# Cross attention and experts: the second tile's softmax and values behind the first tile's outputs, and an earlier first query

## The reference, cut to what matters

```python
def mem_cross_attention(hn, mem_n, wq, wkv, wo):       # 4 heads of 256
    q = hn @ wq;  k, v = split(mem_n @ wkv, 2)
    p = softmax(einsum('bshd,bmhd->bhsm', q, k) * 256 ** -0.5)
    o = einsum('bhsm,bmhd->bshd', p, v).reshape(bsz, seq, D_MODEL)
    return o @ wo

def peer_ffn(hn, wq, subkeys, u_tab, v_tab):           # 8 heads, 2 x 128 subkeys of width 128
    q = (hn @ wq).reshape(T, 8, 2, 128)
    s = einsum('thpd,hpkd->thpk', q, subkeys)
    s1, i1 = top_k(s[:, :, 0], 16);  s2, i2 = top_k(s[:, :, 1], 16)
    top_s, pos = top_k(s1[..., :, None] + s2[..., None, :], 16)   # over the 256 pairs
    idx = (i1 * 128 + i2) at pos;  gate = softmax(top_s)
    act = gelu(einsum('td,thkd->thk', x, u_tab[idx]))
    return einsum('thk,thkd->td', gate * act, v_tab[idx])

h = h + mem_cross_attention(rms_norm(h), mem_n, ...)
h = h + peer_ffn(rms_norm(h), ...)
```

## Time and profile before

| | |
|---|---|
| median of 3 runs | 3084.23 us |
| lowest, highest | 3083.57, 3088.27 us |
| the profiled execution | 3088.53 us, span 3086.8 us |
| mean granted PE clock | 0.938 |
| PE, weight loads, DVE, ACT, POOL busy | 85%, 62%, 69%, 35%, 19% of the span |
| moved by DMA | 810.85 MB; gathers 536.90 MB |

### The profile page before, as it was taken

One profiled execution on the slowest core, in us unless ns is written; L12 is line 12 of the kernel. 1 busy time (PEld: TensorE's weight loads), 2 busy tenths in 40 slices (PEclk: granted clock), 3 DMA queues, 4 the chain that ended last, 5 costly groups with the idle time before them and its releaser, 6 DMA issues. The chain is left out here.

```text
span 3086.8 us, 36100 instructions
## 1 busy us (share of the span) xinstructions
PE 2616.6 (85%) x13122; PEld 1901.4 (62%) x13122; DVE 2116.7 (69%) x4141; ACT 1090.1 (35%) x1973; POOL 599.8 (19%) x547
## 2 busy tenths in 40 slices
PE   8988999998899999899887676668999897667675
PEld 7957998895799797788543222225888653222222
DVE  6457664646766567453889888866664789888875
ACT  4355444435444365444212111113644321112111
POOL 0000000000000000000445444441000254444442
PEclk9999999999999999999998888888999998888888
DMA  6422554552355443143999999997434799999996
GB/s 252 170 96 96 176 184 141 205 175 72 110 181 186 145 153 135 70 164 130 392 427 415 427 426 427 426 426 308 156 122 157 298 425 420 427 426 427 427 426 282
DMA packets 112498, 810.85 MB, mean 263 GB/s; under 512 B 12736, under 2 KB 12736, under 8 KB 14272
## 3 DMA queue, kind: packets, MB, share of 16 engines
q0 software_dynamic: 73728, 536.90, 41.4%
q1 hardware_dynamic: 38592, 271.63, 24.6%
HBM read 807.44 MB, written 1.05 MB: 262 GB/s over the span
## 5 line engine op out<-in xcount | busy, mean ns | idle before, releaser
L3336 PE MATMUL ps<-arena 128*128 128x512 f32 x912 | 533.3, 737 | 240.4 <-ACT arena L3232 236.9
L166 DVE TENSOR_TENSOR ring_low<-ring,parts 128x2048 fp32r<-128x2048 f32 x216 | 492.0, 2291 | 323.9 <-ACT parts L160 320.3
L457 PE MATMUL ps<-parts,parts 128*128 128x256 f32 x2528 | 570.3, 283 | 13.4 <-DVE ring_low L166 10.0
L3336 PEld LDWEIGHTS ps<-arena 128*128 128x128 f32 x912 | 205.4, 235 | 553.9 <-ACT arena L3232 318.6
L457 PE MATMUL ps<-parts,ring_low 128*128 128x256 f32 x1824 | 513.1, 281 | 0.0
L160 ACT ACTIVATE parts<-ring 128x2048 fp32r<-128x2048 f32 x216 | 410.5, 1913 | 270.4 <-PE ps L465 109.5
L465 PE MATMUL ps<-parts,parts 128*128 128x512 f32 x1344 | 439.5, 396 | 7.3 <-DVE ring_low L166 5.3
L457 PEld LDWEIGHTS ps<-parts,parts 128*128 128x128 f32 x2528 | 428.6, 189 | 16.4 <-issue 10.8
L3059 POOL DMA_INDIRECT arena<-in_experts,stage_index x276 | 327.8, 1188 | 536.8 <-PE ps L3336 253.9
L3107 DVE CUSTOM_DVE_ANT_0 arena<-arena 128x1024 f32<-128x1024 f32 x276 | 334.1, 1227 | 95.7 <-DMA arena<-in_experts,stage_index 92.9
L3336 PE MATMUL ps<-ring,arena 128*128 128x512 f32 x616 | 313.0, 645 | 96.8 <-ACT arena L3232 94.2
(11 more groups left out here) (490 smaller groups left out, 2971.5 us busy)
## 6 DMA issues: line engine op xcount, KB each, us to landing
ring<-in_stream SPq DMA_DIRECT2D x249, 1024.0 KB, 4.8
arena<-in_experts,stage_index POOLq DMA_INDIRECT x276
ring<-in_experts,stage_index POOLq DMA_INDIRECT x236
gain_row<-in_gain_rows SPq DMA_DIRECT2D x4, 512.0 KB, 5.9
arena<-in_mem SPq DMA_DIRECT2D x2, 1024.0 KB, 5.6
arena<-in_stream SPq DMA_DIRECT2D x2, 1024.0 KB, 8.5
par<-in_params SPq DMA_DIRECT2D x4, 386.0 KB, 5.0
x<-in_x SPq DMA_DIRECT2D x1, 1024.0 KB, 6.3
```

Of the source, the lines that this page charges most:

```text
L166: dve.tensor_tensor(k.ring_low[v % SLOTS], whole, self.high_of(v).bitcast(F32), ALU.subtract).then_inc(self.ph.sem("chunk_split"), 1)
L457: last = pe.matmul(self.ps[:, 2 * pair + f // 2, (f % 2) * T:(f % 2 + 1) * T], w[:, f * P:(f + 1) * P], x[:, k, :], start=(k == 0 and i == ...
L3336: last = pe.matmul(k.ps[:, bank + n, :], diag[:, s % ROWS, :], rows[row_of[s]][:, D + n * BLK:D + (n + 1) * BLK], start=(s % SLOTS_PER_TOK ...
```

## The change

It applies to both layers.

- On PE the scores, the turn and the values of tile 1 move behind work of tile 0: the scores of tile 1 come after the values of tile 0, its turn inside `outputs(0)`, its values after `outputs(0)` and half of the query product. The query product of tile 0 (`ask_first`, `ask`) stands around the values of tile 1, no longer between blocks of `outputs(1)`; `first_scores` comes after 2 blocks of `outputs(1)` instead of 7.
- ACT and DVE follow: exponentials, maximum and scaling of tile 1 stand behind the result of tile 0 and its third chunk of weights, and the first tile's norm stands in `cross_attention` in front of the result of tile 1.
- Behind the outputs PE asks the second half of the quarter for tile 0 alone, then turns tile 1, and asks the whole quarter for tile 1 in one piece. Before, it turned tile 1, asked the second half for both tiles, then the first half for tile 1.
- On ACT the rest of tile 0's query and the turned copies of tile 1 stand ahead of the squares of tile 1.
- PSUM banks for the turned x go by tile now, and some tiles of the arena lie elsewhere.

```diff
     def bank(self, i, m):
-        at = (i % 2) * T + m * P
-        return self.kern.ps[:, 4 + i // 2, at:at + P]
+        return self.kern.ps[:, 4 + 2 * m + i // self.HALF, (i % self.HALF) * P:(i % self.HALF + 1) * P]
...
 def cross_attention(...): tensor
                 for kt in range(KT):
-                    if (m, n, kt) in expert_early:
-                        expert_early[m, n, kt](pe)
+                    if (m, n, kt) == (0, 1, 2):
+                        turn(1)
+                    if (m, n, kt) == (0, 1, 4):
+                        early.turn_first(pe)
+                    if (m, n, kt) == (1, 0, 2):
+                        early.first_scores(pe)
...
         scores(0)
-        scores(1)
         k.linear_group(pe, ph, lv, (mem_high, mem_low), False, None, split, 0)
         turn(0)
-        turn(1)
         k.linear_group(pe, ph, lv, (mem_high, mem_low), False, None, split, 1)
-        pe.wait_ge(ph.sem("v_copied"), 2)
         values(0)
+        scores(1)
+        outputs(0)
+        early.ask_first(pe)
         values(1)
-        for m in range(MT):
-            outputs(m)
+        early.ask(pe)
+        outputs(1)
...
 def cross_attention(...): scalar, from the exponentials
+        exps(0)
+        split.high_for(act, lv, 0)
+        take_values(0)
+        take_turned(0)
+        split.high_for(act, lv, 1)
+        take_values(1)
+        out_high(0)
+        split.high_for(act, lo, 0, 1)
+        exps(1)
         split.high_for(act, lo, 1, 0)
         k.root_table(act)
+        early.scalar_first(act)
+        take_turned(1)
+        early.scalar_second(act)
+        out_high(1)
...
 def cross_attention(...): vector, from the maximum
+        maximum(0)
+        split.low_for(dve, lv, 0)
+        scale(0)
+        split.low_for(dve, lv, 1)
+        out_low(0)
+        maximum(1)
+        split.low_for(dve, lo, 0, 1)
+        scale(1)
+        early.vector_first(dve, link)
         split.low_for(dve, lo, 1, 0)
+        early.vector_second(dve, link)
+        out_low(1)
...
+class Early:
+    def vector_first(self, dve, link):
+        self.first_added(dve, 0)
+        link(dve.memset(self.z.index, 0.0))
+        self.norm.begin_mean(dve, link)
+    def vector_second(self, dve, link):
+        self.first_added(dve, 1)
+        self.norm.mean(dve, link, 0)
+        self.norm.finish(dve, link, 0)
+    def scalar_first(self, act):
+        self.norm.half_squares(act, 0)
+    def scalar_second(self, act):
+        self.norm.make_whole(act, 0, 0)
+        self.norm.half_squares(act, 1)
+        self.norm.make_whole(act, 0, 1)
+        self.norm.root(act, 0)
+    def ask_first(self, pe):
+        self.k.linear_piece(..., range(0, 4), range(0, 2), self.norm, None, toks=slice(0, P), first=False)
+        self.norm.turn(pe, 0, 1)
+    def ask(self, pe):
+        self.k.linear_piece(..., range(4, KT), range(0, 2), self.norm, "query_parts", toks=slice(0, P), first=False)
...
 def experts(...): scalar
         copy_scores(0, [0, 1])
-        norm.squares(act)
+        rest_of_query()
         norm.make_whole(act, 1, 0)
         norm.make_whole(act, 1, 1)
+        norm.squares(act)
+        copy_scores(0, [2, 3])
         norm.root(act, 1)
         exponentials(0)
-        rest_of_query()
-        copy_scores(0, [2, 3])
         second_tile_query()
...
 def experts(...): tensor
-        pe.wait_ge(ph.sem("scores_copied"), 1)
+        pe.wait_ge(norm.x_added, 3)
+        queries(0, fs=range(2, 4), done="query_parts", toks=first_tile, frees=False)
         norm.turn(pe, 1, 0)
         norm.turn(pe, 1, 1)
-        queries(0, fs=range(2, 4), done="query_parts", frees=False, after=KT)
         some_scores(0, range(2, 4), 2)
-        queries(0, fs=range(0, 2), toks=second_tile, frees=True, first=False, after=KT)
+        queries(0, toks=second_tile, first=False, after=KT)
         some_scores(1, range(0, 4), 3)
```

102 lines of the change are left out of this document (39 added, 63 removed).

## The result

The changed kernel took 3100.43 us (median of 6 runs, 3096.64 to 3102.09) beside 3084.36 for the kernel before (6 runs). The ratio is 1.0047, with a 95% interval of 1.0037 to 1.0057: 11 to 18 us slower. The forecast was 3091.6 us, its range ended at 3096. The direction was right and the size was not.

A forecast was written before the change was run, and what follows sets the result against it. It took the DMA stream of expert gathers as the bound, with buffer releases hanging on PE's first sum and DVE. Lateness of 2 x 3.7 = 7.4 us on the 3084.2 us median gave 3091.6 us; 8-in-10 range 3081 to 3096.

The forecast's parts named there:

- First gather 2.3 us nearer, outputs 1.2 us later: Scores to outputs on PE: first scores and first gather 2.3 us earlier (1.5 to 3), outputs of tile 1 end 1.2 later.
- DVE's mean 3.7 us late: Behind the outputs: DVE's mean of tile 1 waits for ScalarE's squares, at 1479.2 instead of 1475.54; bounds 2.5 and 5 us.
- PE's first sum at 1496.5: Start of expert row sums on PE: late with DVE's first weights, 1496.5 instead of 1492.77, after about 11 us idle.
- The hole: DMA stream before the eleventh gather's data: a gap of about 4 us, with 2 or 3 more around 1516 to 1524.
- Eleven gathers must wait for PE's first sum: Gather buffers: freeing those for gathers nine and ten 3.6 us early is worth nothing, as eleven gathers wait anyway.
- Nothing gives it back: Rest of each expert stage: DMA share stays 1.01, so the nineteenth gather's 3.7 us lateness is the stage's lateness.
- My upper bound of 5 us for the mean: DVE's mean of tile 1: at most 5 us late, if the outputs end 1 us later still.
- The earlier start: Rival: the first gather's earlier start sets the stage's end, each stage 2.3 us shorter, 3079.6 us; chance 0.13.
- The slow clock: Rival: PE's half clock lasts longer after the pause, up to 2.5 us more a layer, 3096.6 us; chance 0.10.
- Partly absorbed: Rival: the eleventh to eighteenth gathers catch up, 1 to 3 us a layer come back, middle 3087.6 us; chance 0.25.

The follow-up runs named there:

- squares_first: Changed kernel with ScalarE's squares of tile 1 ahead of the copy of tile 0's remaining query: 3086.52 us (1.0005) on chip 13, 3093.93 on chip 7.
- tail_before: Changed kernel's first half, with PE's and ScalarE's order of the kernel before behind the outputs of tile 1: 3085.54 us, 0.9998.
- warm: Changed kernel with 16 idle matmuls in PE's pause ahead of the first row sums: 3094.34 us, 1.0031.
- turns_first: Changed kernel with the two turns of tile 1 ahead of tile 0's remaining query on PE: 3093.41 us, 1.0020.
- root_early: Changed kernel with ScalarE's squares and square root of tile 1 ahead of the copy of tile 0's remaining query: 3087.46 us, 1.0006.
- add_behind: root_early with the pairs of the first unit ahead of the second half of tile 1's sum on DVE: 3087.26 us, 1.0006.
- add_behind_padded: add_behind with one harmless one-column copy a layer added on ScalarE: 3086.47 us, 1.0005.
- squares_late: Changed kernel with ScalarE's squares behind the copies of tile 0's last scores and tile 1's query: 3103.74 us (1.0057) on chip 13, 3115.36 on chip 7.

## Why the prediction was wrong, step by step

- **First gather 2.3 us nearer, outputs 1.2 us later.** Measured 2.1 and, from S to the query behind them, 69.3 instead of 67.9 us: 1.4. Right.
- **DVE's mean 3.7 us late.** This is the step that failed. The mechanism was right: ScalarE in strict order, squares behind the query's copy and the turned copies, and DVE's wait named <-ACT L710 in the trace. But the mean stood 6.9 us late (S + 80.1 instead of 73.3). I let the copy start when PE's query ended. It started 3.3 us later, by the held signal, a term that the sum had at nothing. Less these 3.3, the lateness is 3.6 us, the forecast's term. Why the signal is held stays open.
- **PE's first sum at 1496.5.** 1497.94 in an execution that began 1.2 us earlier: against S 6.4 us late instead of 3.7. PE's pause in front of it was 8.6 and 10.2 us, where some 11 were forecast. From the first gather to the nineteenth it took 59.6 us, not 57.
- **The hole.** Forecast at 4 us and 2 or 3 more, less the 2.3 us of earlier start. Measured 8.0 and 9.0 us less stream than before over the same 57 us. (An earlier sentence of the prediction, "Eleven gathers must wait for PE's first sum", is a slip: by the earlier trace rows the eleventh and those behind it wait.)
- **Nothing gives it back.** True of the two layers' sum at large doses (the rule of 2L less 2 us): the sums were 2 x 6.4 us late, the time 14.5 us longer. For one layer it isn't shown, as layer 0 took 4.7 us more and layer 1 8.8. For small doses it isn't either: squares_first's sum was 1.7 us late in each layer and its time moved by 1.5 us in all, but its interval (0.9996 to 1.0014) holds 3.4 us as well as nothing.
- **The rivals.** The earlier start is refuted by tail_before. The slow clock was real (6.04 us for the first sums, 3.70 when kept busy), but it did not last longer than before by more than the kernel before varies, and warm did not show its gain in time. "Partly absorbed" pointed the wrong way.
- **The range** ended at 3096. It took the copy's release as certain, so it had no term for a wait that the trace of before does not show. My upper bound of 5 us for the mean would have needed to be 7.

That the direction came out right is no luck, as the order alone costs time; that the term for it fits to 0.1 us is an inference from one subtraction. With the signal on time, the mean's lateness would then have been the forecast's. The changed kernel itself never ran on chip 13, so that it would have come near 3091 there is an inference, from turns_first (3093.4, squares 77.1 behind S) and from what the signal costs squares_first (7.4 us). That the order alone costs time is shown: turns_first had no held signal and was 1.0020, 1.0010 to 1.0030, while squares_first on the same chip was 1.0005, 0.9996 to 1.0014.

No version beat the kernel before: the best five, tail_before, squares_first on chip 13, root_early, add_behind and add_behind_padded, are all within 0.1% of it.

## What to carry to other kernels

Before you start a stage earlier, ask what frees the buffers of its second round: here the first gather could come 2.1 us earlier for nothing, since the eleventh waited for a sum that waited for the end of the outputs. On an engine in strict order, put what another engine waits for (squares and root) ahead of what hangs on a third engine's signal: with the signal held on one and the same chip, that made 1.0006 of 1.0039. Look for every such product, for the exponentials left behind the copy took what DVE won next. And when a wait is released by nothing that the trace names, try the same program on a second chip before looking for the cause in the program.

## What the hardware showed that I had not expected

- On four of the five numbered chips, and in the changed kernel's first profile, ScalarE got the signal of the query's matmuls up to 3.4 us after their modelled end, at a fixed moment 11.5 to 11.7 us behind the first gather; in the changed kernel the signals of three matmuls then came within 0.12 us. On chip 13 two of the same programs (squares_first, squares_late) had it within 0.1 us. The cause is open.
- The kernel before took 3085 to 3086 us on all of them, while squares_first differed by 7.4 us and squares_late by 11.6. So a change can have two true values, here by chip or by something that went with it.
- Sixteen idle matmuls kept PE's granted clock at 1.00 over a pause in which it had fallen to 0.50, and the eight records of row sums behind it took 3.70 us instead of 6.04.
